# The first attention's outputs made transposed by pairs of heads, in a two-block transformer kernel

## The chip, the cores and the metric

One core of a Trainium2 chip runs the whole program. The metric is the device time of one execution in microseconds (us). Before the change it is 1799.81 us, the median of three runs (1799.48 to 1800.25). The profiled execution took 1798.04 us by the same clock, and its span in the trace is 1796.2 us.

## The reference, cut to what matters

512 tokens of width 1024 pass through one hybrid attention layer and then two recurrent/latent-attention layers with feed-forward parts. The change lies in the first layer only:

```
o_nsa  = g[..., 0:1]*o_cmp + g[..., 1:2]*o_sel + g[..., 2:3]*o_win     # 8 heads of 64
o_nsa  = o_nsa.reshape(B, S, 512) * silu(z_n)
o_dsa  = dsa_branch(...).reshape(B, S, 512) * silu(z_d)               # 8 heads of 64
mixed  = concatenate([o_nsa, o_dsa], -1)
return x + einsum('bsc,cd->bsd', mixed, w_out)
```

With 512 tokens the selected and the window branch both see every earlier token, so `o_sel` and `o_win` are plain causal attentions with different keys and values; `o_cmp` attends to 31 compressed keys; `o_dsa` is causal attention with a top-128 mask. `g` is a gate for each token, head and branch. All is float32.

## The kernel before, in words

Five instruction streams are written by hand (SyncE loads, GpSimd, ScalarE, VectorE, TensorE), each in program order, tied by semaphores. `known` holds the semaphore values of a first pass. Weights arrive as one stream of 1024-column slots into a ring of seven (`RAW`). ScalarE copies a slot to its high part (`WH`, L597), GpSimd subtracts to get the low part (`WL`, L513), and TensorE makes every dense product as three fp32r matmuls of 512 columns (L1914 to L1916). Slots of kind `ada` are not split: they are multiplied by a vector and summed, eight of them in the first attention by ScalarE and GpSimd (L801, L527), the others by VectorE (L1045, L1048). GpSimd advances the `passed` counter strictly in the order of the stream, so that it can make the low part of a slot only after all `ada` slots ahead of it are summed (L518). `stream_order` (L74 on) gives that order.

The first attention is one loop over 96 units (`UNITS1`): branch (selected, window, top-k), head, and query tile `qt` of 128 tokens, which sees `qt + 1` key tiles. For the first two branches the order is branch, head pair index, `qt`, key group; for the third it is `qt` first. In step u of the loop:

- TensorE makes the scores of unit u (L2195, mask L2200 or L2203) into a bank of PSUM;
- VectorE takes the row maximum (L1514), ScalarE the exponential with the row sum (L821) into `PR`;
- TensorE turns the weights of unit u-3 (`T_LAG`, L2210), ScalarE or for every fourth unit VectorE moves them to SBUF (`PT1`, L605 and L1523);
- TensorE makes the output of unit u-4 (`O_LAG`, L2222): tokens on partitions, 64 columns, one matmul for each key tile.

Eight outputs fill a bank. `evict_outputs` (L1480 on) then scales them by gate over row sum into `MIX` (L1506, L1501 and L1503 for the second branch). The compressed branch is done at steps 32 to 64 (`CMP_START`), and its product is added into `MIX` (L2188, L1570). After the loop GpSimd multiplies `MIX` by `Z`, the gate silu(z) (L574), TensorE turns `MIX` by eight blocks (L2012), ScalarE and VectorE make its high and low part (`HH` L839, `HL` L1576), and the output projection `o1` follows: eight dense products of 24 matmuls (L1914 on), with 16 `ada` slots in the stream between their weights. VectorE adds each to `X` (L1582), ScalarE squares it (L617) and GpSimd sums the squares (L537) for the next norm.

Of the kernel before, what the change touches and what calls it, by code (L numbers as in the profile page):

```python
# [33 lines left out]
ALU = mybir.AluOpType  # L34
# [7 lines left out]
P = 128  # L42
D = 1024
# [26 lines left out]
def stream_order():  # L70
# [9 lines left out]
    for n in range(KD):  # L80
        order.append(("o1", n))
        order += [ada.pop(0) for _ in range((2, 3, 3, 3, 3, 2, 0, 0)[n])]
# [75 lines left out]
def mod_points():  # L158
# [27 lines left out]
    "read_act", "full", "ca", "read_dve", "gmix", "h_hi", "lru_par", "lru_w", "topk", "iscore", "cos_sin",  # L186
# [12 lines left out]
CMP_START = (32, 40, 48, 56)  # L199
CMP_MASK, CMP_EXP, CMP_NORM, CMP_TURN, CMP_MOVE, CMP_PV, CMP_ADD = 0, 1, 2, 5, 5, 8, 8  # L200
# [4 lines left out]
TOPK_UNITS = tuple(range(2, 56, 6))  # L205
# [19 lines left out]


def evictor(v):

    return "read_dve" if v % 4 == 3 else "read_act"
# [5 lines left out]
def program(nc, a, known):  # L235

    note = {}
    with ExitStack() as ctx:
# [45 lines left out]
        def w(name, shape, dt, kb):  # L284
# [5 lines left out]
             3: w("G3", [P, NT, 512], F32, 16), 4: w("G4", [P, NT, 512], F32, 24)}  # L290
# [5 lines left out]
        Z = w("Z", [P, NT, D], F32, 32)  # L296
# [23 lines left out]
        MIX = w("MIX", [P, NT, D], F32, 8)  # L320
        PTC = w("PTC", [P, 2, 256], F32, 48)
        PT1 = w("PT1", [P, RING, S], F32, 52)
        GATHER = w("GATHER", [P, S], F32, 72.25)
        RSUM1 = w("RSUM1", [P, 16], F32, 74.5)
        COEF1 = w("COEF1", [P, 8], F32, 74.625)
# [5 lines left out]
        PR = w("PR", [P, RING, S], F32, 0)  # L331
# [100 lines left out]
        def first_square(k):  # L432

            return (RELU[:, 0, :], RELU[:, 1, :], TMP[:, 0, :], TMP[:, 1, :])[k % 4]

# [45 lines left out]
        def _(pool):  # L481
# [68 lines left out]
            for kv in range(2):  # L550

                pass_through(("p1", (4, 2)[kv], 3))
# [17 lines left out]
            pass_through(("o1", 0), 0)  # L570
            for qt in range(NT):
                pool.wait_ge(sem["read_dve"], value("read_dve", "o8", 8 + qt))
                pool.wait_ge(sem["read_act"], value("read_act", "p1", 6, qt))
                nc.gpsimd.tensor_tensor(MIX[:, qt, :], MIX[:, qt, :], Z[:, qt, :], ALU.mult).then_inc(  # L574
                    sem["gmix"], mark("gmix", qt))
# [10 lines left out]
        def _(act):  # L586
# [103 lines left out]
            def evict_group(g):  # L690

                split_through(("p1", g, 3), 0 if g in (2, 3, 6) else SPLIT_RING - 1)
                if g == 0:
                    act.wait_ge(step, value("rstd", "n1"))
                for tt in range(NT):
# [9 lines left out]
                    elif g < 5:  # L705
# [7 lines left out]
                        evict(G[g][:, tt, :], "p1", g, tt, func=ACT.Identity, scale=rstd)  # L713
                    else:
                        act.wait_ge(sem["iscore"], value("iscore", 3, 3))
                        evict(Z[:, tt, (g - 5) * 512:(g - 4) * 512], "p1", g, tt, func=ACT.Silu, scale=rstd)

# [86 lines left out]
            for u in range(len(UNITS1) + T_LAG):  # L804
                if u in O1_SPLITS:
                    split_through(("o1", O1_SPLITS.index(u)), 0)
                v = u - T_LAG
                if v >= 0 and evictor(v) == "read_act":
                    if v >= RING:
                        act.wait_ge(sem["full"], value("full", "o", 1, v - RING))  # L810
                    evict(PT1[:, v % RING, 0:(UNITS1[v][3] + 1) * P], "t", 1, v)
                if u < len(UNITS1):
                    n = (UNITS1[u][3] + 1) * P
                    act.wait_ge(sem["nmax"], value("nmax", 1, u))
                    if u >= RING:
                        act.wait_ge(sem["full"], value("full", "t", 1, u - RING))
                    act.wait_ge(sem["full"], value("full", "s", 1, u))
                    b = bank_of("s", 1, u)
                    if u >= 16 and u % 8 == 0:
                        act.wait_ge(step, value("coef1", u // 8 - 2))  # L820
                    nc.scalar.activation(PR[:, u % RING, 0:n], b[:, 0:n], ACT.Exp, bias=nmax[:, u % 8:u % 8 + 1],  # L821
# [8 lines left out]
                if qt is not None:  # L830
                    if qt >= 2:
                        act.wait_ge(sem["full"], value("full", "cpv", qt - 2))
                    evict(PTC[:, qt % 2, :], "ct", qt)
                if u in ATT_ADA:
                    scale_ada(ATT_ADA.index(u))
            for i in range(KD):
                act.wait_ge(sem["full"], value("full", "tm", i))
                b = bank_of("tm", i)
                nc.scalar.activation(HH[:, i, :], b[:], ACT.Copy).then_inc(sem["mix_hi"], mark("mix_hi", i))  # L839
# [183 lines left out]
        def _(dve):  # L1023
# [456 lines left out]
            def evict_outputs(e):  # L1480

                br, j, _, qt = UNITS1[8 * e]
                dve.wait_ge(sem["read_act"], value("read_act", "s", 1, 8 * e + 7))
                V.reciprocal(COEF1[:], RSUM1[:, 8 * e % 16:8 * e % 16 + 8]).then_inc(step, 1)
                dve.wait_ge(step, own())
                note[("coef1", e)] = count["step"]
                if br < 2:
                    cc = COEF1[:].rearrange("p (t g) -> p t g", g=2)
                    V.tensor_tensor(cc, cc, gate[:, :, 0:24].rearrange(
                        "p t (g c) -> p t g c", g=2)[:, :, :, 3 * j + 1 + br], ALU.mult).then_inc(step, 1)  # L1490
                    dve.wait_ge(step, own())
                    dst = MIX[:, :, 0:512].rearrange("p t (g j d) -> p t g j d", g=2, j=4)[:, :, :, j, :]
                else:
                    dst = MIX[:, qt, 512:1024].rearrange("p (g j d) -> p j g d", g=2, j=4)
                shape = "p (t g d) -> p t g d"
                cc = COEF1[:].rearrange("p (t g o) -> p t g o", t=4, o=1).broadcast_to([P, 4, 2, DH])
                dve.wait_ge(sem["full"], value("full", "o", 1, 8 * e + 7))
                b = bank_of("o8", e)[:].rearrange(shape, t=4, g=2)
                if br == 1:
                    part = GATHER[:].rearrange(shape, t=4, g=2)  # L1500
                    V.tensor_tensor(part, b, cc, ALU.mult).then_inc(sem["read_dve"], mark("read_dve", "o8", e))  # L1501
                    dve.wait_ge(sem["read_dve"], value("read_dve", "o8", e))
                    V.tensor_tensor(dst, dst, part, ALU.add).then_inc(step, 1)  # L1503
                    dve.wait_ge(step, own())
                else:
                    V.tensor_tensor(dst, b, cc, ALU.mult).then_inc(sem["read_dve"], mark("read_dve", "o8", e))  # L1506

            nU = len(UNITS1)
            for u in range(nU + O_LAG):
# [6 lines left out]
                v = u - T_LAG  # L1516
                if 0 <= v < nU and evictor(v) == "read_dve":
                    n = (UNITS1[v][3] + 1) * P
                    dve.wait_ge(sem["full"], value("full", "t", 1, v))
                    b = bank_of("t", 1, v)  # L1520
                    if v >= RING:
                        dve.wait_ge(sem["full"], value("full", "o", 1, v - RING))
                    V.tensor_copy(PT1[:, v % RING, 0:n], b[:, 0:n]).then_inc(  # L1523
                        sem["read_dve"], mark("read_dve", "t", 1, v))
# [1012 lines left out]
```

## Time and profile before

| | |
|---|---|
| median of three runs | 1799.81 us |
| profiled execution, its time and its span | 1798.04 us, 1796.2 us |
| busy TensorE / VectorE / ScalarE / GpSimd | 1734.0 / 990.4 / 741.2 / 692.6 us |
| first attention, first score matmul to last output matmul | 199.19 to 363.0 us |
| first matmul of the output projection | 372.45 us |
| first matmul of the sum of squares behind it | 424.81 us |

The busy times are sums over the span, engine by engine; the last three lines are places in the trace, in us from the start of the span. A matmul's duration in the trace reaches beyond the moment when the next can start, so costs of TensorE are best read from one start to the next.

### The profile page before, as it was taken

To read this page: it belongs to the slowest core of one execution; us is meant where nothing else is said; L and a number is where in the kernel's file an instruction comes from. 1 tells how busy PE (TensorE), PEld (TensorE's weight loads), DVE (VectorE), ACT (ScalarE), POOL (GpSimd) and SP (SyncE) were. 2 spreads that over 40 slices of the span, in tenths; PEclk is the share of its full clock that TensorE was granted. 3 is DMA by queue.
4 is the path that set the end of the run, shared out by engine and by line. 5 is a ranking of instruction groups with operands and counts; after the bars stand their busy time and mean duration, and the time that the engine had idled before them with its cause. 6 is when DMAs were issued, how large, how long until landed. Compare 5 with 4: busy or idle time off the path is not lost. (4 is left out here: it accounts for less than half of the span.)

```text
span 1796.2 us, 23296 instructions
## 1 busy us (share of the span) xinstructions
PE 1734.0 (97%) x8345; PEld 1413.7 (79%) x8345; DVE 990.4 (55%) x1657; ACT 741.2 (41%) x1282; POOL 692.6 (39%) x301
## 2 busy tenths in 40 slices
PE   7999998988999999999999999999999999999997
PEld 7777787777888777788888888887776888888886
DVE  5999776475579687633333335789785631111112
ACT  6434555623375564322222223466464343222321
POOL 3424111236430234555545557440212544444442
PEclk9999999999999999999999999999999999999998
DMA  7234010053332224355555532332311222232211
GB/s 251 81 106 141 24 36 24 25 198 121 105 105 95 81 85 155 133 193 190 194 188 198 189 141 94 107 103 84 105 36 36 94 94 97 92 105 94 97 56 47
DMA packets 56633, 197.65 MB, mean 110 GB/s; under 512 B 6993, under 2 KB 8017, under 8 KB 56530
## 3 DMA queue, kind: packets, MB, share of 16 engines
q1 hardware_dynamic: 55666, 194.15, 31.8%
q10 hardware_dynamic: 864, 2.11, 0.3%
q8 instruction: 67, 1.10, 0.3%
q14 instruction: 36, 0.29, 0.1%
HBM read 194.14 MB, written 2.10 MB: 109 GB/s over the span
## 5 line engine op out<-in xcount | busy, mean ns | idle before, releaser
L513 POOL TENSOR_TENSOR WL<-RAW,WH 128x1024 fp32r<-128x1024 f32 x234 | 594.4, 2546 | 870.8 <-ACT WH L597 529.8
L1914 PE MATMUL bank<-HH,WH 128*128 128x512 f32 x1120 | 437.2, 390 | 9.5 <-POOLq L518 5.9
L1916 PE MATMUL bank<-HH,WL 128*128 128x512 f32 x1120 | 435.9, 389 | 0.0
L1915 PE MATMUL bank<-HL,WH 128*128 128x512 f32 x1120 | 435.8, 389 | 0.0
L597 ACT ACTIVATE WH<-RAW 128x1024 fp32r<-128x1024 f32 x259 | 270.6, 1052 | 244.2 <-PE bank L1916 220.0
L1914 PEld LDWEIGHTS bank<-HH,WH 128*128 128x128 f32 x1120 | 210.2, 188 | 55.1 <-issue 8.8
L1916 PEld LDWEIGHTS bank<-HH,WL 128*128 128x128 f32 x1120 | 210.2, 188 | 43.9
L1915 PEld LDWEIGHTS bank<-HL,WH 128*128 128x128 f32 x1120 | 210.3, 188 | 43.2
L1834 DVE TENSOR_TENSOR HF<-SILU,bank 128x512 f32<-128x512 f32 x43 | 29.6, 688 | 301.6 <-PE bank L1916 300.7
L1914 PE MATMUL bank<-HDH,WH 128*128 128x512 f32 x352 | 137.1, 389 | 0.0
L1916 PE MATMUL bank<-HDH,WL 128*128 128x512 f32 x352 | 136.9, 389 | 0.0
L1915 PE MATMUL bank<-HDL,WH 128*128 128x512 f32 x352 | 136.9, 389 | 0.0
L1914 PE MATMUL bank<-WH,HH 128*128 128x512 f32 (+2 forms) x288 | 112.0, 389 | 13.8 <-DVE WL L1265 8.5
L1845 DVE SCALAR_TENSOR_TENSOR X<-bank,mod,X 128x512 f32<-128x512 f32 x32 | 24.0, 751 | 175.0 <-PE bank L1916 175.0
L1915 PE MATMUL bank<-WL,HH 128*128 128x512 f32 (+2 forms) x288 | 110.3, 383 | 0.0
L1916 PE MATMUL bank<-WH,HL 128*128 128x512 f32 (+2 forms) x288 | 110.3, 383 | 0.0
L1048 DVE SCALAR_TENSOR_TENSOR ACC<-RAW,vec,ACC 128x1024 f32<-128x1024 f32 x70 | 106.7, 1524 | 4.0
L1008 ACT ACTIVATE HDH<-HF 128x512 fp32r<-128x512 f32 x44 | 27.8, 632 | 191.6 <-DVE HF L1834 190.8
L527 POOL TENSOR_TENSOR ACC<-ACC,RAW 128x1024 f32<-128x1024 f32 x14 | 33.7, 2406 | 133.9 <-ACT RAW L801 133.9
L605 ACT ACTIVATE SILU<-bank 128x512 f32<-128x512 f32 x43 | 25.7, 597 | 129.5 <-PE bank L1916 129.5
L1514 DVE TENSOR_REDUCE nmax<-bank 128x1 f32<-128x128 f32 (+3 forms) x96 | 45.9, 489 | 57.4 <-PE bank L2203 37.0
L1916 PEld LDWEIGHTS bank<-HDH,WL 128*128 128x128 f32 x352 | 66.1, 188 | 13.8
(371 smaller groups left out, 2934.5 us busy)
## 6 DMA issues: line engine op xcount, KB each, us to landing
RAW<-in_stream SPq DMA_DIRECT2D x363, 512.0 KB, 3.3
out_t<-YA SPq DMA_DIRECT2D x8, 256.0 KB, 2.2
X<-in_xt ACTq DMA_DIRECT2D x3, 512.0 KB, 10.9
RAW<-in_stream SPq DMA_DIRECT2D x2, 256.0 KB, 3.9
X<-in_xt ACTq DMA_DIRECT2D x2, 256.0 KB, 6.0
ACC<-in_pos SPq DMA_DIRECT2D x1, 256.0 KB
gains<-in_gains SPq DMA_DIRECT2D x1, 224.0 KB
CS<-in_cs SPq DMA_DIRECT2D x1, 128.0 KB
```

Source lines behind the costliest of these rows:

```text
L513: nc.gpsimd.tensor_tensor(lo(k)[:], raw(k)[:], hi(k)[:].bitcast(F32), ALU.subtract).then_inc(sem["passed"], mark("passed", *k))
L527: nc.gpsimd.tensor_tensor(acc, acc, raw(k)[:], ALU.add).then_inc(sem["ada_sum"], mark("ada_sum", i))
L597: nc.scalar.activation(hi(k)[:], raw(k)[:], ACT.Copy).then_inc(sem["w_hi"], mark("w_hi", *k))
L605: return nc.scalar.activation(dst, b[0:dst.shape[0], 0:n], func, **kw).then_inc(sem["read_act"], mark("read_act", *key))
L1008: nc.scalar.activation(HDH[:, f % FH, :], HF[:, f % 2, :], ACT.Copy).then_inc(sem["hid_hi"], mark("hid_hi", L, f))
L1048: ins = V.scalar_tensor_tensor(out=acc, in0=raw(k)[:], scalar=c, in1=acc, op0=ALU.mult, op1=ALU.add)
L1514: V.tensor_reduce(nmax[:, u % 8:u % 8 + 1], b[:, 0:n], AX_X, ALU.max, negate=True).then_inc(sem["nmax"], mark("nmax", 1, u))
L1834: V.tensor_tensor(HF[:, f % 2, :], SILU[:, f % 2, :], b[:], ALU.mult).then_inc(sem["hid"], mark("hid", L, f))
L1845: ins = V.scalar_tensor_tensor(out=X[:, n, :], in0=b[:], scalar=mod[:, L, 5 * KD + n:5 * KD + n + 1], in1=X[:, n, :], op0=ALU.mult, op1=AL ...
L1914: nc.tensor.matmul(out, A[0], B[0], start=first, stop=False)
L1915: nc.tensor.matmul(out, A[0], B[1], start=False, stop=False)
L1916: return nc.tensor.matmul(out, A[1], B[0], start=False, stop=last)
```

## The change: what it does

Order and grouping. The units now run head by head: for each head the selected branch's four query tiles, then the window branch's; then the third branch head by head. Four units of one head and branch are a group, 24 in all. `T_LAG` becomes 6 and `O_LAG` 7, the ring of `PR` grows from four buffers to eight.

Scaling. VectorE takes the reciprocal of each unit's row sum by itself, one step later. GpSimd multiplies the unit's weights in `PR` by it and by the gate (one `tensor_scalar` for each of 96 units) before TensorE turns them.

Outputs. For each group TensorE makes four matmuls, one for each key tile: stationary are 128 columns of `VZ` (the values of a head beside 64 columns of zeros, so that the result lands on one half of the partitions), moving are the turned weights of all later query tiles (512, 384, 256, 128 columns). Both branches of two heads (third branch: two heads) add up in one bank, features on partitions. The compressed branch's product is added to the same bank by one matmul of 512 columns for each pair of heads.

Gate. TensorE turns `Z` in eight blocks in steps 2 to 9, ScalarE moves them back into `Z`. VectorE multiplies a finished bank by the turned gate (`mix_pair_out`), ScalarE and GpSimd or VectorE make the high and low parts during the loop. Only the last block is left for behind it. Nothing is turned after the loop.

Projection. The first two dense products of `o1` are made in parts in steps 101 and 102, their last eighths after the last output. The 16 `ada` slots behind stand four each after `o1` 2 to 5 (before: 2, 3, 3, 3, 3, 2 after `o1` 0 to 5).

Moved: the compressed branch from steps 32 to 64 to steps 2 to 19, the top-k rounds of the third branch from steps 2 to 50 to steps 20 to 60. Before the loop GpSimd clears `VZ` (13 x 64 x 4 columns), and ScalarE writes the values in two instructions for a tile in place of one.

```diff
-UNITS1 = [(b, j, g, qt) for b in (0, 1) for j in range(4) for qt in range(NT) for g in range(2)]
-UNITS1 += [(2, j, g, qt) for qt in range(NT) for j in range(4) for g in range(2)]
+UNITS1 = [(b, h % 4, h // 4, qt) for h in range(HEADS) for b in (0, 1) for qt in range(NT)]
+UNITS1 += [(2, h % 4, h // 4, qt) for h in range(HEADS) for qt in range(NT)]
+NSA_UNITS = 2 * HEADS * NT
+RING1, T_LAG1, O_LAG1 = 8, 6, 7
...
+def mover(v):
+    return "read_dve" if v >= 20 and v % NT == 0 else "read_act"
+MIX_HI = {66: 0, 69: 1, 72: 2, 78: 3, 97: 4, 98: 5, 99: 6}
+MIX_LO_POOL = {66: 0, 69: 1, 72: 2, 77: 3}
+MIX_LO_DVE = {98: 4, 99: 5, 100: 6}
+O1_PASS = (76, 82, 90)
+O1_PARTS = {101: ((0, 0, 3),), 102: ((0, 3, 7), (1, 0, 7), (0, 7, 8), (1, 7, 8))}
+GATE_TURN = 2
-CMP_START = (32, 40, 48, 56)
+CMP_START = (2, 6, 10, 14)
-TOPK_UNITS = tuple(range(2, 56, 6))
+TOPK_UNITS = tuple(range(20, 64, 5))
@@ GpSimd: the loop, in place of the low part of o1 0 and of the products MIX x Z @@
+            for v in range(len(UNITS1)):
+                pool.wait_ge(sem["p_inv"], value("p_inv", v))
+                p_, over = PR[v % RING1][:, 0:n], COEF1[:, v % 16:v % 16 + 1]
+                if br == 2:
+                    ins = nc.gpsimd.tensor_scalar(p_, p_, over, None, ALU.mult)
+                else:
+                    ins = nc.gpsimd.tensor_scalar(p_, p_, over, gate[:, qt, col:col + 1], ALU.mult, ALU.mult)
+                ins.then_inc(sem["p_pool"], mark("p_pool", v))
+                if v - 1 in ATT_ADA:
+                    pass_to(SLOT[("ada", 0, ATT_ADA.index(v - 1))] + 1)
@@ ScalarE: turned gate in steps 3 to 10, then the move of unit u-6, then the exponential of unit u @@
+                v = u - T_LAG1
+                if v >= 0 and mover(v) == "read_act":
+                    if e >= 2:
+                        act.wait_ge(sem["full"], value("full", "o", 1, e - 2))
+                    act.wait_ge(sem["full"], value("full", "t", 1, v))
+                    nc.scalar.activation(PT1[:, e % 2, 0:qt + 1, qt * P:(qt + 1) * P],
...
@@ VectorE: maximum of unit u, then @@
+                v = u - 1
+                    dve.wait_ge(sem["read_act"], value("read_act", "s", 1, v))
+                    V.reciprocal(COEF1[:, v % 16:v % 16 + 1], RSUM1[:, v % 16:v % 16 + 1]).then_inc(
+                        sem["p_inv"], mark("p_inv", v))
+            def mix_pair_out(c):
+                dve.wait_ge(sem["full"], value("full", "oc", c))
+                V.tensor_tensor(gated(c), bank_of("oc", c)[:].rearrange("p (t q) -> p t q", t=NT), gated(c),
                                ALU.mult)
@@ TensorE @@
-                    pe.wait_ge(sem["read_act"], value("read_act", "s", 1, v))
+                    pe.wait_ge(sem["p_pool"], value("p_pool", v))
...
+                    for kb in range(NT):
+                        last = nc.tensor.matmul(
+                            pair_bank[c][:, kb * P:S], VZ[:, kb, DH * m:DH * m + P], PT1[:, e % 2, kb, kb * P:S],
+                            start=(kb == 0 and NT * e == first),
...
+                for n, k0, k1 in O1_PARTS.get(u, ()):
+                    o1_part(n, k0, k1)
-            pe.wait_ge(sem["gmix"], value("gmix", NT - 1))
-            for i in range(KD):
-                turn(("tm", i), [MIX[:, tt, i * P:(i + 1) * P] for tt in range(NT)])
```

## Rows read from the trace of the kernel before

**Rows 1.** The page, part 1: busy us, share of the span, instructions.

```profile
PE 1734.0 (97%) x8345; PEld 1413.7 (79%) x8345; DVE 990.4 (55%) x1657; ACT 741.2 (41%) x1282; POOL 692.6 (39%) x301
```

**Rows 2.** Windows (sum: 199 to 363): length, busy PE, PEld, DVE, ACT, POOL, clock, DMA.

```profile
240.00:250.00 10.00, 10.00 (x83) 8.63 (x82) 6.51 (x17) 6.55 (x19) 2.35 (x1) 1.00 0.13 45
270.00:280.00 10.00, 9.76 (x69) 9.13 (x70) 4.41 (x12) 5.32 (x16) 0.20 (x1) 0.83 0.00 1
...
sum 164.00, PE 156.99 PEld 126.13 DVE 98.28 ACT 96.25 POOL 26.37; mean PE 9.81 PEld 7.88 DVE 6.14 ACT 6.02 POOL 1.65
...
363.00:372.45 9.45, 6.23 (x32) 6.23 (x33) 4.07 (x7) 3.74 (x7) 2.34 (x1) 0.64 0.00 0
```

**Rows 3.** Waits of TensorE in the loop (199 to 363): total, times, longest.

```profile
PE bank L2210 <- ACT PR L821: 2.9, 3, 1.5
PE bank L2179 <- DVE PC L1563: 1.6, 1, 1.6
```

**Rows 4.** Timeline from the last outputs to the first projection matmul: start, duration.

```profile
360.90 2.05 PE L2222 MATMUL bank<-G,PT 128*128 128x64 f32 x16
...
363.83 2.34 POOL L574 TENSOR_TENSOR MIX<-MIX,Z 128x1024 f32<-128x1024 f32 x1 [12.17 <-DVE MIX L1506]
366.22 6.47 PE L2012 MATMUL bank<-ident,MIX 128*128 128x128 f32 x32 [3.27 <-POOL MIX L574]
...
372.45 0.47 PE L1914 MATMUL bank<-HH,WH 128*128 128x512 f32 x1
```

**Rows 5.** Timeline of VectorE and TensorE in the projection.

```profile
374.24 0.75 DVE L1045 TENSOR_SCALAR ACC<-RAW,vec 128x1024 f32<-128x1024 f32 x1
...
424.81 0.58 PE L2022 MATMUL bank<-ones,SQ 128*128 128x1 f32 x4
```

**Rows 6.** Waits in the projection (372 to 440).

```profile
PE bank L1914 <- POOLq L518: 5.6, 3, 2.5
```

**Rows 7.** Timeline: the same unit (qt 1) of two rounds of eight.

```profile
222.23 0.65 PE L2195 MATMUL bank<-KT,QNT 128*128 128x256 f32 x2
...
234.04 0.65 PE L2195 MATMUL bank<-KT,QNT 128*128 128x256 f32 x2
```

**Rows 8.** Timeline of one unit of four key tiles.

```profile
349.39 0.60 PE L2210 MATMUL bank<-ident,PR 128*128 128x128 f32 x4
349.59 0.69 DVE L1514 TENSOR_REDUCE nmax<-bank 128x1 f32<-128x512 f32 x1 [0.37 <-PE bank L2200]
349.83 1.00 PE L2222 MATMUL bank<-G,PT 128*128 128x64 f32 x8
350.09 0.60 ACT L605 ACTIVATE PT<-bank 128x512 f32<-128x512 f32 x1 [0.92 <-PE bank L2210]
350.58 0.68 ACT L821 ACTIVATE PR<-bank,nmax 128x512 f32<-128x512 f32 x1
350.67 1.08 PE L2195 MATMUL bank<-KT,QDT 128*128 128x512 f32 x2
```

**Rows 9.** Timeline of the second attention: one head's output, four matmuls, and what follows.

```profile
658.85 2.41 PE L2353 MATMUL bank<-PT,V 128*128 128x512 f32 x8
...
660.98 0.30 PEld L2333 LDWEIGHTS bank<-KN,QN 128*128 128x128 f32 x2
```

**Rows 10.** Timeline of ScalarE: the first exponential, an `ada` slot.

```profile
201.08 0.37 ACT L821 ACTIVATE PR<-bank,nmax 128x128 f32<-128x128 f32 x1
...
230.36 1.14 ACT L801 ACTIVATE RAW<-RAW,vec 128x1024 f32<-128x1024 f32 x1
```

**Rows 11.** Groups of GpSimd by form: busy, mean ns of one.

```profile
L537 POOL TENSOR_TENSOR SQ<-SQT 128x512 f32<-128x512 f32 x5 | 7.4, 1486 | 2.1 <-ACT SQT L617 2.1
L544 POOL MEMSET VBLK<- 128x512 f32 x1 | 0.5, 525 | 0.0
```

**Rows 12.** Timeline in the projection: VectorE beside GpSimd.

```profile
419.93 2.42 POOL L513 TENSOR_TENSOR WL<-RAW,WH 128x1024 fp32r<-128x1024 f32 x1
...
420.20 2.16 DVE L1062 TENSOR_TENSOR mod<-mod,par 128x8 f32<-128x8 f32 x1
```

More of the change, by code:

```diff
@@ L81, in stream_order @@
         order.append(("o1", n))
-        order += [ada.pop(0) for _ in range((2, 3, 3, 3, 3, 2, 0, 0)[n])]
+        order += [ada.pop(0) for _ in range((0, 0, 4, 4, 4, 4, 0, 0)[n])]
     for layer in range(LAYERS):
@@ L330, in program @@
         KT = at("KT", [P, 6, S], F32, 32 * KB)
-        PR = w("PR", [P, RING, S], F32, 0)
+        PR = [w(f"PR{i}", [P, S], F32, kb) for i, kb in enumerate((0, 2, 4, 6, 54, 56, 69.25, 72.25))]
         PC = at("PC", [P, 2, 8, NCMP], F32, 44 * KB)
@@ L1477, in _ @@
                 V.tensor_copy(QDT[:, i, :], b[:]).then_inc(sem["read_dve"], mark("read_dve", "tqd", i))
[L1480 to L1506, printed above, removed]
@@ L1508, in _ @@
+            pair_at = {pair_done(c) + 1: c for c in range(KD)}
             nU = len(UNITS1)
-            for u in range(nU + O_LAG):
+            for u in range(nU + O_LAG1):
                 if u < nU:
@@ L1564, in _ @@
                                     ALU.mult).then_inc(sem["cmp_p"], mark("cmp_p", qt))
[L1565 to L1577 removed]
+            mix_pair_out(KD - 1)
+            mix_low(KD - 1)
             for n in range(KD):
@@ L2124, in _ @@
             pe.wait_ge(sem["read_act"], value("read_act", "p1", 4, 3))
-            turn(("tc", 1), [G[4][:, tt, 384:512] for tt in range(NT)])
+            turn(("tc", 1), [VC[:, tt, :] for tt in range(NT)])
             project(3)
@@ L2182, in _ @@
                     full(last, "ct", qt)
-                qt = cmp_tile(u, CMP_PV)
-                if qt is not None:
-                    pe.wait_ge(sem["read_act"], value("read_act", "ct", qt))
-                    b = claim("cpv", qt)
-                    for g in range(2):
-                        last = nc.tensor.matmul(b[:, g * 256:(g + 1) * 256], PTC[:, qt % 2, g * P:(g + 1) * P],
-                                                VBLK[:, g, :], start=True, stop=True)
-                    full(last, "cpv", qt)
                 if u < nU:
@@ new lines, in _ @@
+                for c in range(4):
+                    if u == pair_done(c):
+                        if c == 0:
+                            pe.wait_ge(sem["read_act"], value("read_act", "ct", NT - 1))
+                        full(nc.tensor.matmul(pair_bank[c][:], VBLK[:, c // 2, P * (c % 2):P * (c % 2) + P],
+                                              PTC[:, c // 2, :], start=False, stop=True), "oc", c)
+                for n, k0, k1 in O1_PARTS.get(u, ()):
+                    o1_part(n, k0, k1)
@@ L2235, in _ @@
+            banks[0] = 8
             for n in range(KD):
-                dense(("o1", n), [(("o1", n), P * k) for k in range(KD)], mix_pair)
+                if n > 1:
+                    dense(("o1", n), [(("o1", n), P * k) for k in range(KD)], mix_pair)
                 mods(("o1", n))
```

212 lines of the change are left out of this document (132 added, 80 removed).

## The prediction

> **What bounds the kernel now.** I read the page's busy times first: TensorE works 97% of the span and no other engine over 55% [rows 1]. So time can only come from places where TensorE waits, runs at the lower clock, or does less work. I then cut the stretch that the change touches into windows. From 240 to 250 TensorE is busy 10.00 of 10.00 us although ScalarE, VectorE, a top-k round and an `ada` slot work beside it; over the whole loop it is busy 156.99 of 164, so 7.0 us are idle, and in 270 to 280 the mean granted clock is 0.83, part of it at 1.2 instead of 2.4 GHz, which costs 10 x 0.17 = 1.7 us more [rows 2]. So the loop loses 8.7 us. The list of waits puts the idle time where the compressed branch runs: 1.6 us on VectorE's product and 2.9 us on exponentials [rows 3]. Behind the loop lies the largest hole: the last outputs end at 362.95, GpSimd multiplies the last tile of `MIX` until 366.17, the 32 turns begin at 366.22 and the projection at 372.45 [rows 4], and that stretch has a mean clock of 0.64 [rows 2]. The projection then takes 424.81 - 372.45 = 52.4 us up to the sum of squares [rows 4, 5], of which 5.6 are waits for GpSimd, which may not pass the `ada` slots before VectorE has summed them [rows 6].
>
> **Step 1, behind the loop.** GpSimd's product, the 32 turns and the high and low parts go from behind the last output: 372.45 - 362.95 = 9.5 us less. Instead only block 7 remains: a product of VectorE, a copy of ScalarE and a difference of VectorE, 0.69 + 0.60 + 0.69 and three hand-overs, some 2.3 us. TensorE has 12 + 21 matmuls to do first; (52.4 - 5.6 - 1.8 for 16 small turns) / 192 = 0.234 us each, so 7.7 us cover it. The nine matmuls in step 101 are the same work earlier. The same projection, so 52.4 us, kept.
>
> **Step 2, the `ada` slots.** VectorE can begin them 2.4 us after the last output, where now it begins 374.24 - 362.95 = 11.3 us after it [rows 5]. That looks like a gain, but all four slots before `o1` 3, 4, 5 and 6 must be summed before GpSimd makes that low part, and VectorE takes an `ada` slot only after it has added the earlier `o1` tile to `X`. Following it through, `o1` 3 is in time, `o1` 4 late by 2 to 3 us, `o1` 5 by up to 1, `o1` 6 by 3 to 4. I keep the 5.6 us of waits; bounds 3 and 9.
>
> **Step 3, work added to the loop.** The 32 turns of `Z` cost what turns cost at full clock: four start at 349.39 and the outputs at 349.83 [rows 8], 0.11 us each, 3.5 us. An output group: before, ten key tiles, 0.84 us for four (349.83 to 350.67) [rows 8], 2.10 us. After, the same shape as a head of the second attention: 658.85 to 660.98, 2.13 us [rows 9], or 2.24 if the next matmul's start is taken. 24 groups: +0.7 to +3.4, I take +2.0. The compressed product has as many columns as before. Together +5.5 us.
>
> **Step 4, who feeds TensorE now.** Here the waits decide. In a half round of four units TensorE needs 11.81 / 2 = 5.9 us [rows 7]. Outputs now come in one lump of 2.13 us, one step after the turns of the largest tile. The chain from the end of the scores of `qt` 3 to that lump: 0.20 until VectorE starts, 0.69, the exponential 0.68 with 0.03, the move of `qt` 2 about 0.4, the exponential of `qt` 0 0.37, the move of `qt` 3 0.60 with 0.05 [rows 8, 10]: 3.0 us. TensorE meanwhile has ten turns (1.1) and the three smaller scores (5.9 - 1.1 - 2.1 - 0.95 for the largest, 1.75): 2.85 us. So 16 groups wait about 0.13 each, 2 us; in the third branch the longer mask closes this. Bounds 0 (as from 240 to 250) and 0.3 x 24 = 7. What is queued behind this wait is the next score, and with it VectorE and ScalarE, so it does not heal by itself. The `ada` slots on ScalarE (1.14 each [rows 10]) fall into this chain in steps 31, 40 and 67: 2 of 3.4 us taken, bounds 0 and 5 with the top-k rounds at 35 and 55. At the start the turned weights come three steps later, the first exponential starts only at 201.08, 1.9 us after the first scores [rows 10], and steps 2 to 9 hold the gate's turns and two compressed tiles, with ScalarE to clear a bank for nearly each claim: per step 0.49 for the gate, as much for the move and 0.37 to 0.68 for the exponential, against some 1.6 of TensorE. I take 3 us lost; bounds 0 and 6. Sum of waits 7 us, ends 0 and 18, against 8.7 lost before.
>
> GpSimd's new multiplication is in no row. Nearest are its difference with two inputs, 1.49 us for 512 columns (2.9 ns a column), and its clearing, 0.525 us (1.0 ns) [rows 11]. A group has 1280 columns: 1.3 to 3.7 us of 5.9, so it hides, and the six steps between scores and turn hold its delay; it decides only above 5.9 / 1280 = 4.6 ns. The rows alone leave that possible, since none has a scalar operand. By the Trainium skill (GPSIMD Engine Reference, section 3.1) one-input work there costs about one cycle an element, by my estimate 0.9 ns a column, and two-input work 2.6 cycles; by that page this stays hidden, and my chance for the rival below is small.
>
> Against the change speaks that GpSimd now works beside VectorE: a product of eight columns took 2.16 us while a GpSimd difference of 2.42 us ran [rows 12]. The Trainium skill (SBUF — State Buffer, Who interferes with whom) says that a VectorE instruction with two SBUF inputs and a GpSimd one that reads SBUF lock each other out. In the loop VectorE has eleven such (eight of the compressed branch, three low parts), each of which could wait up to one multiplication of at most 1.5 us; eight lie in the start phase, which is part of its upper bound.
>
> **Sum.** 9.5 less behind, 5.5 more work, waits 8.7 to 7: 9.5 - 5.5 + 1.7 = 5.7 us less. The profiled execution took 1798.04, which gives 1792.3; the median of the runs is 1.8 above it, and the forecast for that median is **1794.1 us**. Before the loop I count nothing: clearing 3328 columns at 1.0 ns takes GpSimd 3.4 us once beside dense matmuls.
>
> **The rivals.** (a) The loop waits hardly at all (2 us), as from 240 to 250: 10.7 less, 1789.1. For it: six steps of slack instead of three; against it: that stretch had outputs spread evenly. (b) The waits only move, from the compressed branch's old place to the start and to the lumps: 13 us of them, 1800.1, no change. For it: the 3.0 against 2.85. (c) Slower: in steps 2 to 9 each claim of a bank waits for ScalarE's previous one, about 1 us a step, 8 us, and after this idling TensorE drops to half clock for 6 us as after 362.95 [rows 2], 3 us; with lumps and `ada` slots at 8, 19 us of waits and 1806. It decides from 12.7 us of waits on. For it: ScalarE's and TensorE's work per step are nearly equal there; against it: only eight steps. (d) GpSimd's multiplication costs 5.5 ns a column: 7.0 us a group, 1.1 x 24 = 26 more, 1820 or above. That the projection would not start inside the loop can't be: only block 7 depends on the last output.
>
> **Chances.** Forecast 0.42, (a) 0.17, (b) 0.24, (c) 0.12, (d) 0.05. The forecast and (a) are faster by over 0.2% (3.6 us, about what can be told from no change): 0.59. (b) is within it: 0.24. (c) and (d) are slower: 0.17. The forecast's own range is 1791 to 1797; with (a), (b) and part of (c) 1787 to 1804.
>
> **What would show it.** Step 1: first projection matmul before the last outputs, no idle time and clock 1.00 behind. Step 2: waits on GpSimd's queue in the projection near 5.6 us. Step 3: output groups 2.1 to 2.25 us from start to next. Step 4: TensorE waiting on moves (`PT`) once a group by a tenth or two; idle time of some 3 us in the first 20 us of the loop. Wrong it would be if the loop's lost time were under 3 or over 12 us, or if GpSimd's multiplication ended waits of TensorE.

## The result, and the profile after

The changed kernel is slower. Its median is 1816.32 us (7 runs, 1807.0 to 1820.0) against 1799.48 us for the kernel before (7 runs, 1798.7 to 1801.1): ratio 1.0076, 95% interval 1.006 to 1.0092. Forecast were 1794.1 us and a range of 1787 to 1804; the time lies 12 us outside. The profiled execution took 1816.41 us with a span of 1814.6. Even the spread has grown, from 2.4 to 13 us.

Part 1 of the page answers to [rows 1], and a window over the loop (first score matmul to the start of the last output lump) to the sum of [rows 2]:

```profile
PE 1739.2 (96%) x8049; PEld 1391.7 (77%) x8049; DVE 978.4 (54%) x1712; ACT 749.5 (41%) x1299; POOL 759.5 (42%) x398
```

```profile
207.00:387.00 180.00, 162.71 (x841) 107.34 (x842) 90.75 (x284) 108.50 (x307) 101.36 (x110) 1.00 0.10 33
```

The idle time of TensorE in it is now 17.3 us, where the whole loop before had 7.0. Two timelines place the loss, each by the first score matmul (start, duration, operation, idle time before it and what ended that). First the kernel before, then the one after:

```profile
199.19 0.46 PE L2195 MATMUL bank<-KT,QNT 128*128 128x128 f32 x2 [1.26 <-ACT KCT L780]
...
424.44 0.94 PE L2022 MATMUL bank<-ones,SQ 128*128 128x1 f32 x8
```

```profile
207.11 0.46 PE L2277 MATMUL bank<-KT,QNT 128*128 128x128 f32 x2 [0.90 <-ACT QNT L667]
...
384.88 0.47 PE L1981 MATMUL bank<-HH,WH 128*128 128x512 f32 x1
...
387.04 2.32 PE L2308 MATMUL bank<-PT,VZ 128*128 128x512 f32 x8
389.11 0.48 PE L1981 MATMUL bank<-HH,WH 128*128 128x512 f32 x1
...
389.46 0.69 DVE L1570 TENSOR_TENSOR Z<-bank,Z 128x512 f32<-128x512 f32 x1 [3.37 <-PE bank L2308]
...
441.12 0.95 PE L2089 MATMUL bank<-ones,SQ 128*128 128x1 f32 x8
```

| stretch | before | after | measured | forecast |
|---|---|---|---|---|
| start to first score | 199.19 | 207.11 | +7.9 | 0 |
| first score to end of last output | 163.8 | 182.0 | +18.2 | +5.9 |
| from there to the sum of squares | 61.5 | 52.0 | -9.5 | -11.6 |

In the kernel before, the first matmul of the sum of squares starts at 424.44; the 424.81 of [rows 5] is the start of a later one of the same eight, so that the projection took 52.0 us and not 52.4. The forecast's column has 5.5 - 1.7 + 2.1 and -9.5 - 2.1; the 2.1 are projection matmuls that now run in the loop (384.88 to 387.04). The three measured numbers make +16.6. For the remaining 1.8 us up to the span's +18.4 I have only the granted clock behind these stretches: it is 0.50 from 445 to 448, 708 to 711, 759 to 762 and 1390.5 to 1393.5 us, in the kernel before only from 618 to 621 and 1372 to 1375.

The tail did what it should (389.11 follows the last lump without a gap), and both losses lie where the prediction counted nothing or little. The first is one wait, ahead of the loop; the second is spread over the loop. The list of waits (engine, line, releaser: total, times, longest), from 40 to 110 us, before and after:

```profile
PE bank L1914 <- DVE SCORE L1410: 0.9, 1, 0.9
```

```profile
PE bank L1981 <- DVE SCORE L1496: 7.3, 1, 7.3
```

The clock falls with the wait. TensorE was idle from 85.4 to 92.78, and the granted clock is 0.52 from 92 to 97 us, where the kernel before had 1.00 at the same work (85 to 90 us). In the traces below it is so wherever this wait stands near 7 us, and not where it stays at 0.9 (a1_clear_scalar). The first matmuls behind it, and the one at which they are fast again:

```profile
92.78 0.79 PE L1981 MATMUL bank<-WH,HH 128*128 128x512 f32 x1 [7.34 <-DVE SCORE L1496]
93.38 0.63 PE L1982 MATMUL bank<-WL,HH 128*128 128x512 f32 x1
...
96.79 0.40 PE L1981 MATMUL bank<-WH,HH 128*128 128x512 f32 x1
```

Nine matmuls take 4.0 us here (92.78 to 96.79) and took 2.2 before (85.90 to 88.08). So TensorE is 6.9 us late when the score comes and 8.7 after the slow matmuls; it wins back 0.8 from two waits of the kernel before that are now shorter or gone (0.40 at 107.48, and 1.26 against 0.90 ahead of the first score), which leaves the 7.9.

In the loop, the waits of TensorE and of its weight loader:

```profile
PE bank L2308 <- ACT PT L897: 7.0, 8, 1.4
PE bank L2292 <- ACT PTC L918: 2.5, 3, 0.9
PE bank L2292 <- POOL PR L627: 1.8, 1, 1.8
```

```profile
PEld bank L2308 <- ACT PT L897: 12.1, 18, 1.6
```

L2308 is the output lump, L897 ScalarE's move of the turned weights. The lumps of four units start 6.85 us apart in the mean (229.47 to 387.04, 24 of them). Where no other work falls between them it is 6.15 us, where four units took 5.9 before [rows 7]; over the whole loop four units took 163.8 / 24 = 6.8 us before and take 182.0 / 24 = 7.6 now. That is the wait that the prediction priced at 2 us. One group shows how it comes about (the timeline, all engines, shortened):

```profile
276.40 0.68 DVE L1520 MAX8 TKM<-SQS 128x8 f32<-128x512 f32 x1
276.86 0.61 PE L2292 MATMUL bank<-ident,PR 128*128 128x128 f32 x4
...
277.19 0.68 DVE L1522 MATCH_REPLACE8 SQS<-TKM,SQS 128x512 f32<-128x512 f32 x1
277.30 0.89 PE L2277 MATMUL bank<-KT,QNT 128*128 128x384 f32 x2
...
277.90 0.29 DVE L1587 TENSOR_REDUCE nmax<-bank 128x1 f32<-128x128 f32 x1
...
278.23 0.37 ACT L907 ACTIVATE PR<-bank,nmax 128x128 f32<-128x128 f32 x1 [0.62 <-DVE nmax L1587]
...
278.58 0.59 ACT L897 ACTIVATE PT<-bank 128x512 f32<-128x512 f32 x1
...
279.23 2.42 PE L2308 MATMUL bank<-PT,VZ 128*128 128x512 f32 x8 [0.86 <-ACT PT L897]
```

The fourth tile's turn is over at 277.47. Its move stands in ScalarE's queue behind the exponential of the unit one step before, and that one waits for a maximum that VectorE makes behind a top-k round. So the move ends at 279.17, and TensorE, with only one set of scores and a small turn between turn and lump, waits 0.86 us. (From 342 us on there are no top-k rounds, and the lumps still stand 6.2 to 7.3 us apart, against 6.0 in the run a3_lag8 below, so top-k rounds are not the whole of it.) The next scores come later by as much, and so, I argue, do their maximum and exponential, and the next group begins no better.

### The profile page after: what moved, and what is told of

Read it like the earlier page. It is cut to its first block and busy times, and to the rows that moved or that the text cites. A ratio compares the mean times of both kernels' runs of the same rounds, so it can differ in the third digit from the quotient of the medians.

```text
span 1814.6 us, 22848 instructions
## 1 busy us (share of the span) xinstructions
PE 1739.2 (96%) x8049; PEld 1391.7 (77%) x8049; DVE 978.4 (54%) x1712; ACT 749.5 (41%) x1299; POOL 759.5 (42%) x398
## 5 line engine op out<-in xcount | busy, mean ns | idle before, releaser
L1134 DVE SCALAR_TENSOR_TENSOR ACC<-RAW,vec,ACC 128x1024 f32<-128x1024 f32 x70 | 99.3, 1418 | 4.0
L1587 DVE TENSOR_REDUCE nmax<-bank 128x1 f32<-128x128 f32 (+1 forms) x96 | 46.0, 482 | 62.8 <-PE bank L2285 36.2
L1981 PEld LDWEIGHTS bank<-WH,HH 128*128 128x128 f32 x288 | 55.2, 192 | 32.1 <-DVE WL L1351 8.0
```

Of the source, the lines that this page charges most:

```text
L1134: ins = V.scalar_tensor_tensor(out=acc, in0=raw(k)[:], scalar=c, in1=acc, op0=ALU.mult, op1=ALU.add)
L1587: V.tensor_reduce(nmax[:, u % 8:u % 8 + 1], b[:, 0:n], AX_X, ALU.max, negate=True).then_inc(sem["nmax"], mark("nmax", 1, u))
L1981: nc.tensor.matmul(out, A[0], B[0], start=first, stop=False)
```

## The experiments

Theory: two costs. **T1**, GpSimd's clearing of `VZ` delays VectorE ahead of the loop. **T2**, the output lump, one step behind its last turn, waits for ScalarE's move. Rivals: **T3**, GpSimd's multiplication holds the turn; **T4**, the gate's turns and the compressed tiles crowd the first steps. Each was timed in five or more runs. Times are medians; the kernel before gave 1799.3, 1799.9, 1799.6 and 1799.5 us beside them.

### T1: the clearing

The clearing alone, in the kernel before (b1_clear):

```diff
+                    pool.wait_ge(sem["full"], value("full", "ti", 2))
+                    nc.gpsimd.memset(VZ[:], 0.0).then_inc(sem["pool_set"], mark("pool_set", "vz"))
```

> The kernel before with one thing of the change added: GpSimd clears 128x3328 fp32 (2.9 us) once, after the indexer's third turn and before the projection of group 4 is evicted; its output is unchanged. Theory 1 (the loss of 7.9 us ahead of the loop comes from that clearing, which shifts GpSimd's splits against VectorE's small SBUF instructions where VectorE is the bound): the first score matmul of the loop moves from 199.2 to 203 to 208 us and the whole gets 4 to 8 us longer, 1803 to 1808 us, with a wider spread between runs than the 2.4 us of before. Rival (the clearing is harmless, the loss comes from the rest of the change ahead of the loop, such as the split eviction of group 4): 1799 to 1801 us, first score matmul at 199 to 200.

1805.02 us, ratio 1.0034 (1.0021 to 1.0047); first score at 207.08. One instruction on an idle GpSimd costs 5.7 us, and 7.9 up to the loop; where the other 2.2 are won back is not shown. The spread did not widen. And taken out of the changed kernel (a1_clear_scalar):

```diff
-                    nc.gpsimd.memset(VZ[:], 0.0).then_inc(sem["pool_set"], mark("pool_set", "vz"))
+                    nc.scalar.activation(
+                        VZ[:].rearrange("p t (b d) -> p t b d", d=DH)[:, :, 0:13:2, :],
+                        TKM[:, 0:1].rearrange("p (t b d) -> p t b d", t=1, b=1).broadcast_to([P, NT, 7, DH]),
+                        ACT.Copy)
```

> The changed kernel with the clearing taken from GpSimd: ScalarE writes the zeros, into the seven blocks that stay zero alone (128x1792, about 1.7 us), ahead of its eviction of group 4. Theory 1 (GpSimd's clearing costs the time ahead of the loop): the first score matmul comes at 199 to 202 us instead of 207.1, the whole takes 1807 to 1811 us instead of 1816, and the spread of runs shrinks from 13 us to some 3. Rival (the loss has another cause ahead of the loop): first score matmul at 206 to 209 us, 1815 to 1818 us.

1807.13 us, 9.2 less than the changed kernel; first score at 199.93; its runs spread over 3.0 us. T1 holds from both sides, most firmly by the first score; of the 9.2 us a part may be spread, as two of the changed kernel's seven runs took 1807.0 and 1807.2 us themselves. How it costs is seen in VectorE's and GpSimd's timelines from 57 to 90 us, of the kernel before:

```profile
59.17 2.44 POOL L513 TENSOR_TENSOR WL<-RAW,WH 128x1024 fp32r<-128x1024 f32 x1 [6.22 <-ACT WH L597]
59.39 2.31 DVE L1355 TENSOR_SCALAR TMP<-TMP 128x128 f32<-128x128 f32 x1
63.82 2.32 DVE L1221 TENSOR_REDUCE kst<-HSQ 128x6 f32<-128x384 f32 x4
64.11 2.40 POOL L513 TENSOR_TENSOR WL<-RAW,WH 128x1024 fp32r<-128x1024 f32 x1 [2.50 <-ACT WH L597]
```

and of the changed one (here only the long ones of VectorE, with GpSimd's):

```profile
57.95 2.88 POOL L598 MEMSET VZ<- 128x3328 f32 x1 [4.53 <-PE bank L2079]
59.35 1.56 DVE L1455 TENSOR_SCALAR cs<-TMP 128x128 f32<-128x128 f32 x1
60.80 2.39 POOL L556 TENSOR_TENSOR WL<-RAW,WH 128x1024 fp32r<-128x1024 f32 x1
60.95 2.33 DVE L1439 TENSOR_SCALAR TMP<-TMP 128x128 f32<-128x128 f32 x1
64.16 3.03 DVE L1449 SCALAR_TENSOR_TENSOR TMP<-TMP 128x128 f32<-128x128 f32 x3
64.59 2.45 POOL L556 TENSOR_TENSOR WL<-RAW,WH 128x1024 fp32r<-128x1024 f32 x1 [1.40 <-ACT WH L659]
67.74 2.32 DVE L1307 TENSOR_REDUCE kst<-HSQ 128x6 f32<-128x384 f32 x4
70.09 2.37 DVE L1311 TENSOR_SCALAR kst<-kst 128x24 f32<-128x24 f32 x1
...
84.22 5.15 DVE L1267 SCALAR_TENSOR_TENSOR TAB<-CS,gains 128x128 f32<-128x128 f32 x4
```

VectorE works nearly without a break there, as a window of the kernel before shows (7.45 of 8 us, and 7.75 from 82 to 90):

```profile
58.00:66.00 8.00, 8.00 (x37) 6.62 (x36) 7.45 (x17) 2.15 (x3) 4.33 (x2) 1.00 0.20 66
```

TensorE is busy for all of these 8 us too, and up to 85 us the changed kernel's is only the 0.5 us late that it was at 57 us. But then it needs VectorE's score product, and it waited 0.9 us for that before: VectorE's work up to there had no slack, and what it loses TensorE loses.

A `tensor_scalar` of 128x128 takes 0.23 us alone (L1369 of before) and 2.31 when a GpSimd split runs. Before, the split at 64.11 fell beside sums (L1221, 2.32 for four, as without it); now it falls beside L1449, 3.03 instead of 0.94. Counting the long ones up to the score's product against what the same instructions take undisturbed, before lost 2.1 + 2.2 + 2.2 + 1.1 = 7.6 us, after 1.3 + 2.1 + 2.1 + 2.0 + 2.2 + 4.3 = 14.0. The difference, 6.4, and the 0.5 us by which VectorE is later at 57 us already, make the 6.9 us by which that product comes later. The Trainium skill (SBUF — State Buffer, Who interferes with whom) says that sums never contend, that a VectorE instruction with two SBUF inputs does so only with a GpSimd one that reads SBUF, and that a `tensor_scalar` can take the shared ports and then contends with any. These rows agree, the 1.56 beside the clearing too.

Is it the delay, or the long clearing? The same place in the kernel before, kept busy by 80 small clearings (b2_delay_only):

```diff
-                    nc.gpsimd.memset(VZ[:], 0.0).then_inc(sem["pool_set"], mark("pool_set", "vz"))
+                    for i in range(79):
+                        nc.gpsimd.memset(VZ[:, i // 20, 8 * (i % 20):8 * (i % 20) + 8], 0.0)
+                    nc.gpsimd.memset(VZ[:, 3, 152:160], 0.0).then_inc(sem["pool_set"], mark("pool_set", "vz"))
```

> The kernel before, with GpSimd kept busy at the place of the clearing by 80 clearings of 128x8 one after another (from the distance of the small ones at the program's start, 0.03 us each, about 2.8 us in all), which write a fifth of the columns in slices too short to hold anything up for long; the output is unchanged. Theory (the clearing costs by delay: it puts GpSimd's next split from 59.2 to 60.8 us, onto other of VectorE's small instructions): as with the full clearing, first score matmul at 204 to 208 us, 1803 to 1807 us. Rival (the long clearing itself, by holding up the VectorE instruction beside it, starts the chain): 1799 to 1801 us, first scores at 199 to 201.

```profile
58.06 2.77 POOL L557 MEMSET VZ<- 128x8 f32 x79 [4.53 <-PE bank L2021]
...
59.46 1.49 DVE L1378 TENSOR_SCALAR cs<-TMP 128x128 f32<-128x128 f32 x1
60.83 2.40 POOL L514 TENSOR_TENSOR WL<-RAW,WH 128x1024 fp32r<-128x1024 f32 x1
60.99 2.32 DVE L1362 TENSOR_SCALAR TMP<-TMP 128x128 f32<-128x128 f32 x1
```

1806.79 us, first score at 207.28. By time the theory is confirmed, but the row at 59.46 shows that my premise was wrong: the small clearings held VectorE up just as long (1.49 against 1.56). So neither one long instruction nor all the columns are needed, 2.8 us of GpSimd are enough; whether by the hold of 1.3 us or by the split's delay of 1.6 stays open.

### T2: the lump

One step more between the turn and the lump (a3_lag8, from the changed kernel, GpSimd's clearing kept):

```diff
-RING1, T_LAG1, O_LAG1 = 8, 6, 7
+RING1, T_LAG1, O_LAG1 = 8, 6, 8
-O1_PARTS = {101: ((0, 0, 3),), 102: ((0, 3, 7), (1, 0, 7), (0, 7, 8), (1, 7, 8))}
+O1_PARTS = {102: ((0, 0, 3),), 103: ((0, 3, 7), (1, 0, 7), (0, 7, 8), (1, 7, 8))}
```

> The changed kernel with the output lump one step later (8 steps behind its scores instead of 7; the turn stays at 6). Theory 2 (the lump waits for ScalarE's move of a turn issued one step before): the 7 us that the lump waits for ScalarE's moves, and the 12 us of weight loads with it, nearly vanish, the mean distance of lumps falls from 6.85 us to 6.3 to 6.5, the loop from 182 to 172 to 177 us, less one more step of 1.5 us at its end, and the kernel gets 5 to 8 us faster. Rival (the loop is held by the chain through ScalarE and VectorE, exponentials 20 us late, so that a wait taken from the lump comes back at the next score or turn): the waits for the moves go and others of the same size come, the loop stays within 2 us of 182.

1799.20 us (11 runs), ratio 0.9995 (0.9986 to 1.0003): 17.1 us less, more than twice what I expected. First score at 207.97, last lump at 372.23: 164.3 us instead of 179.9. TensorE's wait in the loop, of this kernel:

```profile
PE bank L2308 <- ACT PT L897: 0.4, 1, 0.4
```

and its window:

```profile
208.00:374.00 166.00, 157.63 (x843) 107.19 (x848) 90.56 (x284) 111.05 (x306) 101.01 (x110) 1.00 0.11 36
```

The same work (GpSimd 101.0 against 101.4 us, ScalarE 111.1 against 108.5) in 14 us less, here with the last lump. Groups without extra work are 5.67 us apart. T2 holds, and the rows understated it: 7.0 and 12.1 us of waits, 15.6 gained. TensorE's idle time fell by 8.9 us (17.3 to 8.4), and its busy time, which the waits don't list, by 5.1 more (162.7 to 157.6). That a late lump makes the next maximum and exponential late, and so costs more than its own wait, fits this and is argued.

Can the distance come from the other end (t5_turn_early, from a1_clear_scalar)?

```diff
-RING1, T_LAG1, O_LAG1 = 8, 6, 7
+RING1, T_LAG1, O_LAG1 = 8, 5, 7
```

> On the changed kernel with ScalarE's clearing (1807.1 us, loop 182.2 us from the first scores to the last lump's end): the turn goes 5 steps behind its scores instead of 6, the lump stays at 7, so that two steps instead of one lie between a turn and the lump that needs its move. Theory A (what counts is the distance from turn to lump, because ScalarE's move stands behind an exponential that waits for VectorE): the lump's waits for the moves vanish as with the longer lag, the loop comes to 166 to 170 us, the whole to 1791 to 1796. Theory B (the depth of the whole chain from scores over the maximum, the exponential, the reciprocal and GpSimd to the turn is used up too): the wait moves to the turn, which then waits for GpSimd's multiplication, and the whole stays at 1801 to 1808.

1804.94 us (12 runs, 1798.2 to 1810.1), 2.2 less than 1807.1. The lump's wait falls from 7.0 to 0.9 us, but others come. Of the weight loader, from 198 to 388 us:

```profile
PEld bank L2292 <- POOL PR L623: 6.9, 9, 1.9
...
PEld bank L2277 <- ACT PR L907: 3.0, 15, 0.4
PEld bank L2308 <- ACT PT L897: 2.3, 5, 0.6
PEld bank L2292 <- POOL PR L620: 2.3, 7, 0.7
```

Theory B is the nearer one by the median and by who is waited for. But the first of these waits stood at 6.1 us in a1_clear_scalar already, and the runs differ in clock: the median of their mean granted clocks is 0.990 here and 0.994 there. The three runs at 0.993 and 0.994 took 1798.2 to 1799.3 us, those of a1_clear_scalar at 0.994 and 0.995 took 1805.8 to 1807.1. At an equal clock the gain is some 7 us and lies between the theories. A plain group takes 5.91 us, between 6.15 and the 5.67 of the longer lag: taking the step from the turn's side gives a part of what the eighth step gives.

Is it the queue order? On ScalarE alone the fourth tile's move ahead of the exponential before it (s1_move_first, from a1_clear_scalar):

```diff
-                v = u - T_LAG1
-                if v >= 0 and mover(v) == "read_act":
+                for v in (u - T_LAG1, u - T_LAG1 + 1):
+                    if v < 0 or v >= len(UNITS1) or mover(v) != "read_act" or (v % NT == NT - 1) != (v > u - T_LAG1):
+                        continue
```

> On the changed kernel with ScalarE's clearing (1807.1 us, loop 182 us), lump again 7 steps behind: on ScalarE alone the move of a group's fourth tile goes ahead of the exponential that stood before it in its queue; every other order stays. Theory (the lump waits because that move stands behind an exponential that waits for VectorE's maximum): the lump's waits for the move, 7.0 us by the row, shrink to under 2, and the kernel gets 5 to 12 us faster, 1795 to 1802. Rival (the distance of one step is too short by itself, or the exponential that is now late makes the maximum's bank, the reciprocal and the later turns late): 1804 us or more, with other waits in place of the lump's.

1806.42 us, no gain that can be told. In a plain group it works (the lump at 276.04 has no wait), but the list still has 4.2 us for it, 0.8 of it at 270.18, where the move stands behind an `ada` slot of 1.14 us instead, and the exponentials are late in their turn. From first to last lump it takes 154.3 us against 157.6, but its first score comes at 202.77 instead of 199.93. My sub-theory, that the order alone is at fault, falls: the order is worth 3 us of the loop where a step of slack is worth 15.6.

### T3 and T4

GpSimd's multiplications left out, so that the weights are neither divided by their sums nor gated (n4_no_scale, from a1_clear_scalar):

> On the changed kernel with ScalarE's clearing (1807.1 us): GpSimd's multiplications of the weights are left out (it passes each unit on as soon as the reciprocal is there), so the weights aren't divided by their sums nor gated. Theory 3 (GpSimd's multiplication holds the turn): 8 us and more go, 1799 or less. Rival (the lump waits for ScalarE's move, whatever GpSimd does): 0 to 3 us go, 1804 to 1807, and the waits of the lump for the move stay at 6 to 8 us.

1805.65 us, 1.5 less; the lump's wait is 7.0 us as before. T3 falls, but its rows held a surprise. GpSimd by form in the changed kernel (count | busy us, mean ns | idle before):

```profile
L624 POOL TENSOR_SCALAR PR<-PR,COEF 128x512 f32<-128x512 f32 x8 | 12.5, 1566 | 0.5 <-DVE COEF L1592 0.5
L627 POOL TENSOR_SCALAR PR<-PR,COEF,gate 128x512 f32<-128x512 f32 x16 | 12.5, 779 | 6.0 <-DVE COEF L1592 5.5 <-POOLq L561 0.5
...
L627 POOL TENSOR_SCALAR PR<-PR,COEF,gate 128x128 f32<-128x128 f32 x16 | 7.2, 451 | 14.9 <-DVE COEF L1592 14.6 <-POOLq L561 0.2
```

With one factor it takes twice as long as with two. So (a2_two_factors, from the changed kernel):

```diff
-                    ins = nc.gpsimd.tensor_scalar(p_, p_, over, None, ALU.mult)
+                    ins = nc.gpsimd.tensor_scalar(p_, p_, over, 1.0, ALU.mult, ALU.mult)
```

> The changed kernel with GpSimd's multiplication of the third branch in the form with two factors (the second is 1.0), which took 779 ns at 512 columns in the first two branches against 1566 with one factor. Theory 3 (the slow form fills GpSimd between 330 and 380 us, so that weights come late to the turn): the third branch's 1.9 us a group fall away, GpSimd's busy share there goes from 8.5 to about 6.5 tenths, the output groups 17 to 24 come 0.4 to 0.8 us closer together, and the kernel gets 3 to 6 us faster than the changed kernel. Rival (GpSimd is busy there but the turn waits for it only for the splits and the ada slots): the multiplications get shorter, the whole changes by under 1 us. Second rival: the second factor given as a number instead of a column of SBUF is as slow as one factor, nothing changes.

```profile
L624 POOL TENSOR_SCALAR PR<-PR,COEF 128x512 f32<-128x512 f32 x8 | 5.6, 695 | 2.6 <-DVE COEF L1592 2.6
```

695 ns instead of 1566, and 1815.91 us, no change: GpSimd was busy, not late. The first rival had it, and the second, that a number is slow, is out. The crowding (g12_gate_late, from a1_clear_scalar):

```diff
-CMP_START = (2, 6, 10, 14)
+CMP_START = (8, 12, 16, 20)
-GATE_TURN = 2
+GATE_TURN = 12
```

> On the changed kernel with ScalarE's clearing (1807.1 us): the gate's eight turns go from steps 2 to 9 to steps 12 to 19, and the compressed branch's four tiles start at steps 8, 12, 16, 20 instead of 2, 6, 10, 14. Theory 4 (the first steps are overcrowded: the first lump comes 22.4 us after the first scores where eleven steps of the mean 1.7 us would be 19): the first lump comes 3 us sooner, the later ones keep 1 to 2 us of it, 1804 to 1806 us. Rival (the same work in other steps makes the same waits there): within 1 us of 1807.

1810.47 us, 3.3 more, a miss for both. The first lump comes at 208.55 instead of 222.29, but the fifth at 253.28 instead of 251.86. So the work fits into the first steps better than into later ones, and T4 falls.

### Both mendings, and more

c1_lag8_clear has the diffs of a1_clear_scalar and a3_lag8:

> Both mendings in one kernel: the zeros of VZ written by ScalarE and the output lump 8 steps behind its scores. Theory: the two costs lie in different stages and add up, so the time is that of the lag alone (1799.2) less what the clearing cost before the loop (207.97 - 199.93 = 8.0 us at the first score matmul): 1790 to 1793 us, with first scores at 200 us and a last output at 364 to 366; faster than the kernel before by 0.35 to 0.5%. Rival: the lag also mended something of the clearing's shift (its loop started 8 us late and met the splits and the ada slots at other phases), so that they don't add: 1795 to 1799 us.

1795.49 us (6 runs, 1792.3 to 1800.4), ratio 0.9973 (0.996 to 0.9985): faster than the kernel before, but 4 us short of the sum and within the rival's range. A part lay in the sum: it took the 8.0 us of the first score, while the clearing had cost the whole kernel 5.7 (b1_clear), and with these the sum is 1793.5. The rest is open. Its profiled execution is the slowest of the six, and shows why that one is. First this kernel from 11 to 24 us behind its first score, then a3_lag8 in the same stretch (the number after the five engines is the granted clock):

```profile
211.00:224.00 13.00, 11.19 (x40) 7.86 (x40) 4.71 (x16) 4.99 (x15) 1.98 (x3) 0.50 0.13 41
```

```profile
219.00:232.00 13.00, 9.68 (x65) 6.89 (x65) 6.37 (x22) 7.59 (x22) 2.98 (x5) 1.00 0.12 42
```

The same program part ran 13 us at 1.2 GHz here and at 2.4 there. Ahead of the fall TensorE was busy 9.57 of 11 us, in a3_lag8 9.80 of 11. Why the clock fell in one and not in the other is open; in the profile of c3_lag8_clear_two, below, it fell in the same stretch (0.61 from 211 to 224). The clock goes with the spread: of the six runs the one at a mean granted clock of 0.992 took 1792.3 us, the one at 0.986 1800.4. It does not explain the missing 4 us, since at 0.989 this kernel took 1794.1 and 1796.9 us and a3_lag8 1799.2 and 1799.5, as far apart as the medians are.

c3_lag8_clear_two adds the diff of a2_two_factors:

> The kernel with both mendings (lump 8 steps behind, zeros by ScalarE; median 1795.5 us) and GpSimd's third-branch multiplication in the form with two factors, the second a number (695 ns at 512 columns instead of 1566). Theory (GpSimd's own queue, now the nearest to the bound at the slots of the ada blocks, where the turn of the accumulated row waits 3.0 us for it): 1 to 3 us faster, 1792 to 1795. Rival (it is not in the chain, as at a lag of 7): no change beyond 1 us, 1795 to 1796.

1793.61 us (1791.7 to 1794.7), ratio 0.9962 (0.9948 to 0.9976), the fastest kernel of the study. The wait for the `ada` sum falls from 3.0 to 2.1 us, but its interval overlaps with c1_lag8_clear's and its runs had a granted clock of 0.992 in the median against 0.989, so this last gain is not shown. And nine steps (c1b_lag9_clear):

> As the kernel with both mendings (median 1795.5 us) but with the lump 9 steps behind its scores. Theory (one more step was all that the move needed; the lump's wait is 0.4 us in sum at a lag of 8): no gain, one more step of 1 to 1.5 us at the loop's end, 1795 to 1798. Rival (the loop still loses by depth): 1790 to 1793.

1794.47 us, ratio 0.9968 (0.9956 to 0.998): within 1.0 us of eight steps. Eight are enough.

## Why the prediction was wrong

- **Step 1** was right in its gap: -9.5 forecast, and no gap found. The stretch to the sum of squares came 2.1 us longer than forecast: 0.6 of it are waits, and 1.6 the granted clock of 0.97 where I had expected 1.00 (52 x 0.03; it is 0.50 from 428 to 431 us). The 52.4 us of the kept projection were 52.0, read from a wrong matmul.
- **Step 2** was right: 5.6 us of waits kept, 4.0 + 2.2 = 6.2 measured:

```profile
PE bank L1981 <- POOLq L561: 4.0, 2, 2.3
PE bank L1981 <- POOL WL L556: 2.2, 1, 2.2
```

- **Step 3** was right in its lumps: 2.13 to 2.24 us forecast, 2.16 to 2.26 measured from a lump's start to the next matmul's (2.07 for the last one, 387.04 to 389.11; one took 4.0). Its sum was too high, if anything: the loop of a3_lag8 takes 166.3 us from first score to last output, against 163.8 + 5.9 = 169.7 forecast, although TensorE is idle in it for 8.4 us and not for 7. A group without extra work takes 5.67 us there, under the 5.9 of [rows 7], a saving that the step had not seen.
- **Step 4 failed**, in the term "16 groups wait about 0.13 each, 2 us", upper bound 7. TensorE was idle for 17.3 us of the loop, beyond the 12 us that I had named as a sign of being wrong, and taking this one wait away by a step of slack gave 15.6 us. The chain of 3.0 against 2.85 us was laid from one set of scores to the lump, with each hand-over taken at its undisturbed time. I left out that VectorE's maximum stands behind top-k rounds and that the move then stands behind the exponential that waits for it. I had written that such a wait "does not heal by itself", and still priced each one as if it did. The start was only a small part of the failure: 4.7 us idle up to the first lump (207.00 to 229.47) against 3 forecast, and much the same in a3_lag8, 4.5. The `ada` slots stand in a3_lag8 too.
- **"Before the loop I count nothing" failed** too: +7.9 us. The 3.4 us (2.88 measured) do lie beside dense matmuls, but behind these TensorE waits for VectorE's score product, on a path without slack, and I had read no window of it. The wait then cost 1.8 us of clock besides. The rule of two engines locking each other out was weighed for eleven loop instructions only.
- **Rivals**: (d), GpSimd's multiplication, was rightly small: 0.85 ns a column with two factors ((779 - 451) / 384), 2.5 with one ((1566 - 605) / 384, 605 being its time at 128 columns), under the 4.6 from which it would decide. My estimate of 0.9 ns holds for the form with two factors and not for the one with one. My sign for it did come, one wait of 1.8 us that the multiplication ended, but all of it was worth 1.5 us (n4_no_scale). (b) had a right place, the lumps, with 13 us of waits where 17.3 came. (c) had the sign, but not the place: the loss ran through all 24 groups, not steps 2 to 9. (a)'s 1789.1 was not reached by any kernel here.
- **Range**: it held neither loss. Without the two, the change brings what was forecast of it (1793.6 to 1795.5 against 1794.1), a coincidence in part: the clock took some, and the loop, 3.4 us shorter than forecast, gave some.

## What to carry to other kernels

Where results come in lumps, lay the chain for the last tile of the lump through every queue it passes, with what may stand ahead in each, and give it a step more than the chain says: a step too many cost nothing here that can be told, one too few 15.6 us. Work put on an idle engine costs by what it pushes: find the path without slack near the place where it is put, also if the busiest engine looks covered, and read which instructions of that path slow down beside the idle engine. A term counted at nothing deserves one window of the profile.

## What the runs showed of the hardware

- GpSimd's multiplication of 128x512 by one column takes 1566 ns, by two 779, by a column and the number 1.0 695 (451 and 605 at 128 columns for two and one).
- Small clearings on GpSimd, 0.035 us apart, hold a VectorE `tensor_scalar` up as long as one long clearing (1.49 and 1.56 us instead of 0.23).
- After a wait of 7.3 us TensorE's granted clock was 0.50 for nine matmuls, which took 4.0 us instead of 2.2.
- The spread between runs goes with the mean granted clock of the run. In the changed kernel it is 0.993 at 1807.0 us and 0.988 at 1820.0, in t5_turn_early 0.994 at 1798.2 and 0.987 at 1810.1. GpSimd's clearing doesn't make it: alone in the kernel before it leaves 2.3 us of spread, and t5_turn_early has 11.9 without it. What lowers the clock in one run and not in the next is open.
